# The last expert's rows added by TensorE, and the pair rows loaded behind the weights, at the end of two mixture-of-experts stages

## The reference, cut to what matters

```python
x = x + mixer(rmsnorm(x))
h = rmsnorm(x)
# g: the token's best group of 4; top-2 of the 8 experts in it; weights from both softmaxes
combine[t, expert] = weight
for e in range(32):
    hid = silu(h @ w_gate[e]) * (h @ w_up[e])            # (544, 1024) @ (1024, 256)
    out = out + combine[:, e:e+1] * (hid @ w_down[e])    # (544, 256) @ (256, 1024)
x = x + out                                              # after layer 1: rmsnorm(x) is the output
```

## Time and profile before

| | us |
|---|---|
| median of three runs (1033.27 to 1037.01) | 1036.26 |
| the profiled execution's own time | 1037.41 |
| its span in the trace | 1035.6 |
| layer 0: first gate and up of its expert stage / last copy to `rows_out` / last add to `x_T` ends | 250.49 / 485.07 / 507.81 |
| layer 1: last copy to `rows_out` / last product with the gain ends | 1002.26 / 1032.51 |

### The profile page before, as it was taken

How to read it: one execution, slowest core, us unless ns; L and a number is a source line. 1 busy time by engine, 2 the same in 40 slices (tenths; PEclk the granted TensorE clock), 3 DMA queues, 4 the chain that set the end, 5 groups by cost and what they waited for, 6 DMA issues and landing times. The chain is left out here.

```text
span 1035.6 us, 18796 instructions
## 1 busy us (share of the span) xinstructions
PE 922.1 (89%) x7270; PEld 663.2 (64%) x7270; DVE 413.8 (40%) x955; ACT 287.5 (28%) x595; POOL 293.1 (28%) x438
## 2 busy tenths in 40 slices
PE   7999999977999889876689999989979998898885
PEld 6988888864555555553587878569755555555553
DVE  5266784255111111111768878772561111111115
ACT  6356673241112111110532112362312111111103
POOL 1810000013333343311053527720123343342110
PEclk9999999997999989997699999999979999998997
DMA  8512111778999999995924636315879999999966
GB/s 234 188 37 54 49 42 53 274 293 319 379 416 416 416 414 415 418 418 199 291 67 129 159 85 155 93 43 216 358 278 390 414 417 416 416 416 418 420 270 239
DMA packets 112277, 277.71 MB, mean 268 GB/s; under 512 B 34952, under 2 KB 73176, under 8 KB 88074
## 3 DMA queue, kind: packets, MB, share of 16 engines
q1 hardware_dynamic: 96630, 253.74, 64.4%
q0 software_dynamic: 11424, 17.87, 4.7%
q10 hardware_dynamic: 4132, 4.86, 1.9%
HBM read 266.25 MB, written 27.45 MB: 284 GB/s over the span
## 5 line engine op out<-in xcount | busy, mean ns | idle before, releaser
L2106 DVE COPY areaB<-ps 128x512 f32<-128x512 f32 x66 | 45.6, 691 | 345.9 <-PE ps L2089 345.9
L2072 PE MATMUL ps<-ring,areaB 128*64 128x256 f32 x576 | 143.2, 405 | 20.7 <-issue 16.6
L2073 PE MATMUL ps<-ring,areaB 128*64 128x256 f32 x576 | 143.6, 406 | 0.0
L2118 POOL DMA_INDIRECT pair_rows<-areaB,idx x66 | 67.7, 1025 | 247.7 <-DVE areaB L2106 236.9
L2072 PEld LDWEIGHTS ps<-ring,areaB 128*64 128x64 f32 x576 | 80.9, 146 | 62.5 <-issue 23.1
L2097 ACT ACTIVATE v_rows<-ps 128x256 f32<-128x256 f32 x66 | 25.3, 384 | 257.8 <-PE ps L2073 257.8
L1058 PE MATMUL ps<-conv_x_high,pw_halves 128*128 128x272 f32 x512 | 89.4, 295 | 2.9 <-DVE areaS L1293 2.9
L2113 POOL DMA_INDIRECT areaC<-h_rows,idx x66 | 68.7, 1041 | 60.0 <-issue 45.8
L2094 ACT ACTIVATE areaB<-ps 128x512 f32<-128x512 f32 x66 | 39.3, 597 | 153.5 <-PE ps L2062 153.5
L2073 PEld LDWEIGHTS ps<-ring,areaB 128*64 128x64 f32 x576 | 80.8, 146 | 0.0
L2089 PE MATMUL ps<-ring,areaB 128*64 128x512 f32 x320 | 76.0, 593 | 2.2 <-DVE areaB L2103 1.6
(11 more groups left out here) (381 smaller groups left out, 1930.5 us busy)
## 6 DMA issues: line engine op xcount, KB each, us to landing
ring<-in_w_down SPq DMA_DIRECT2D x40, 1024.0 KB, 23.9
ring<-in_w_gate SPq DMA_DIRECT2D x32, 1024.0 KB, 23.1
ring<-in_w_up SPq DMA_DIRECT2D x32, 1024.0 KB, 26.0
wring<-in_w_down SPq DMA_DIRECT2D x12, 1024.0 KB, 25.0
areaS<-in_w_down SPq DMA_DIRECT2D x12, 1024.0 KB, 27.1
wring<-in_w_pw SPq DMA_DIRECT2D x24, 512.0 KB, 4.5
areaA<-in_w_gate SPq DMA_DIRECT2D x10, 1024.0 KB, 27.1
areaA<-in_w_up SPq DMA_DIRECT2D x10, 1024.0 KB, 29.5
```

Of the source, the lines that this page charges most:

```text
L2072: pe.matmul(ps[0:CAP, 2 + odd, 0:F], rows, ring_gate(ws)[:, k, :], start=(k == 0), stop=(k == KT - 1))
L2073: mm = pe.matmul(ps[CAP:P, 2 + odd, 0:F], rows, ring_up(ws)[:, k, :], start=(k == 0), stop=(k == KT - 1))
L2106: return v.tensor_copy(rows_out[:, s, :], ps[:, 5 + odd, :])
L2118: return gp.indirect_dma_start(pair_half_rows, bass.IndirectOffsetOnAxis(idx[:, RING + s:RING + 1 + s], 0), rows_out[:, s, :], None, bound ...
```

## The change

1. **Tile 32 isn't scattered.** Its 64 rows stay in SBUF (`late_rows`), and TensorE adds them in the combining. For this VectorE, once per layer at tile 10 (`weigh_late`, 20 instructions), takes the pairs of the last expert out of `weight` and builds a matrix from slot to token that holds their weights; TensorE turns it in tiles 12 and 14 (`turn_late`), and ScalarE keeps it in `late_T` (64 slots, twice, by 544 tokens).
2. **Order of the weights.** Down of position 30 is issued ahead of gate and up of position 31, and TensorE does down of tile 31 ahead of gate and up of tile 32 (in layer 1 also `turn_x` of two token tiles).
3. **Pairs behind the weights.** `pair(t)` now lies in weight buffers 0 and 2 alone. SP issues the loads as soon as down of tile 31 is done and the scatters of tiles 0 to 31 have landed (`early_rows_stored`), ahead of the branch for overfull experts.
4. **The combining.** Layer 0: per token tile 8 matmuls add the last expert's rows in PSUM, then 8 matmuls with the identity, in place of 8 transposes, add the mixed row. Layer 1: ScalarE and VectorE mix the two choices of the first four tiles into one row in SBUF (`mix`), TensorE adds stream and last expert in PSUM, VectorE adds both (`add_up`); only the last token tile keeps the product with the diagonal.
5. Since rows of `pair_rows` now stay unwritten, the attention stage fills it once with `x` (six transfers from DRAM to DRAM, 4.25 MB).

```diff
                     for i in range(6, NW):
                         sp.wait_ge(w_ready[i % 2], i // 2)
                         load_weights(sp, i)
+                        if i < 10:
+                            c, a = (i - 6) // 2, (i - 6) % 2
+                            sp.dma_start(pair_rows[c * T + a * NP // 2:c * T + (a + 1) * NP // 2, :],
+                                         x_prompt2[a * NP // 2:(a + 1) * NP // 2, :]).then_inc(pairs_filled, 16)
...
-        pairs = flat[:, 0:NT * 2 * D].rearrange("p (t c n) -> p t c n", t=NT, c=2)
+        pair = lambda t: ring[:, 0 if t < 3 else 2, (t % 3) * 2 * D:(t % 3 + 1) * 2 * D].rearrange("p (c n) -> p c n", c=2)
...
                 def tensor(self, pe):
-                    pe.wait_ge(out_kept, NCH)
-                    for i, t in enumerate(ORDER):
-                        r = rows_of(t)
-                        pe.wait_ge(mixed, i + 1)
+                    def late(i):
...
                         for k in range(KT):
-                            mm = pe.transpose(banks(i)[:, k // 4, (k % 4) * P:(k % 4) * P + r],
-                                              x_rows[0:r, t, k * P:(k + 1) * P], ident[0:r, 0:r])
+                            at = slice(k // 4 * CAP, (k // 4 + 1) * CAP)
+                            pe.matmul(banks(i)[:, k // 4, (k % 4) * P:(k % 4) * P + r], late_rows[at, (k % 4) * P:(k % 4 + 1) * P],
+                                      late_T[at, t * P:t * P + r], start=(k % 4 == 0), stop=False)
+
+                    def turn(i):
+                        t = ORDER[i]
+                        r = rows_of(t)
+                        pe.wait_ge(mixed, i + 1)
+                        for k in range(KT):
+                            mm = pe.matmul(banks(i)[:, k // 4, (k % 4) * P:(k % 4) * P + r],
+                                           pair(t)[0:r, 0, k * P:(k + 1) * P], ident[0:r, 0:r], start=False, stop=(k % 4 == 3))
                         mm.then_inc(turned, 1)
+
+                    pe.wait_ge(late_kept, 2)
+                    pe.wait_ge(out_kept, NCH)
+                    for i in range(4):
+                        late(i)
+                    turn(0)
+                    turn(1)
+                    late(4)
+                    for i in range(2, NT):
+                        turn(i)
...
+                def before_last(self, pe):
+                    self.turn_x(pe, 1)
+                    pe.wait_ge(out_kept, NCH - 1)
+                    self.turn_x(pe, 0)
...
+                        for c in range(2):
+                            at = slice(c * CAP, (c + 1) * CAP)
+                            mm = pe.matmul(banks(i)[0:r, c, :], late_T[at, t * P:t * P + r], late_rows[at, :], start=False, stop=i < NT - 1)
...
                         this = expert
+                        if e + 2 == NE:
+                            next_down(e, this)
                         if e + 1 < NE:
...
-                        next_down(e, this)
+                        if e + 2 != NE:
+                            next_down(e, this)
...
+                    sp.wait_ge(down_done, last)
+                    sp.wait_ge(early_rows_stored, 1)
+                    load_pairs(sp, l)
                     more.sync(sp, spill_of(sp))
-                    sp.wait_ge(rows_complete, 1)
-                    load_pairs(sp, l)
...
-                        store(Tile(e))
-                    spilled = spill_of(gp)
+                        if e < last:
+                            store(Tile(e))
                     for s in range(RROW):
-                        gp.wait_ge(scattered[s], 16 * len(range(s, NCH, RROW)))
-                    more.gpsimd(gp, spilled)
-                    gp.sem_inc(rows_complete, 1)
+                        gp.wait_ge(scattered[s], 16 * len(range(s, last, RROW)))
+                    gp.sem_inc(early_rows_stored, 1)
...
+                        if final:
+                            out(x.shift(-1))
+                            combine.before_last(pe)
...
+                        n.link(v.tensor_tensor(late_weight, late_weight, weight, ALU.mult))
+                        n.done(v.tensor_tensor(weight, weight, late_weight, ALU.subtract))
+                        for c in range(2 * NT):
+                            n.done(v.tensor_scalar(twice[:, c % NT, c // NT, :], slot_no[:, :], rank[:, c:c + 1], late_weight[:, c:c + 1],
+                                                   ALU.is_equal, ALU.mult))
```

More of the change, by code:

```diff
@@ L1972, in turn_x, with scalar, scale_first @@
+                def scalar(self, act):
+                    def scale_first(i):
                         t = ORDER[i]
                         r = rows_of(t)
[L1974 to L1980 removed]
+                        act.wait_ge(landed[t], 16)
+                        nc.scalar.activation(pair(t)[0:r, 0, :], pair(t)[0:r, 0, :], ACT.Copy,
+                                             scale=weight[0:r, t:t + 1]).then_inc(first_scaled, 1)
+                    for i in range(3):
+                        scale_first(i)
@@ L2106, in keep_out, with turn_late @@
                 return v.tensor_copy(rows_out[:, s, :], ps[:, 5 + odd, :])
+            def turn_late(pe, ts):
+                pe.wait_ge(late_step, LATE_STEPS)
+                after(pe, late_kept, ts[0] // 4)
+                for t in ts:
+                    twice = match[0:rows_of(t), 2 * t:2 * t + 2, :].rearrange("p a s -> p (a s)")
+                    mm = pe.transpose(ps[:, 7, (t % 4) * P:(t % 4) * P + rows_of(t)], twice, ident[0:rows_of(t), 0:rows_of(t)])
+                return mm
             def fill_idx(gp, s, e, sem_, of, at):
@@ L2370, in over, with before, behind @@
                                 body(e, NE * j + e, j)
-                def sync(self, sp, spilled):
+                        if behind:
+                            behind()
+                        else:
+                            for t in ORDER:
+                                eng.wait_ge(pairs_landed[l][t], 32)
+                def sync(self, sp, spilled):
+                    def before():
+                        for t in ORDER:
+                            sp.wait_ge(pairs_landed[l][t], 16)
+                    def behind():
+                        sp.wait_ge(o["complete"], 1)
+                        load_pairs(sp, l)
                     def body(e, n, j):
@@ L2376, in body @@
                             sp.dma_start(dst, rows_by_partition(src, l, e)).then_inc(o["landed"], 16)
-                    self.over(sp, spilled, body)
+                    self.over(sp, spilled, body, before=before, behind=behind)
                 def gpsimd(self, gp, spilled):
```

184 lines of the change are left out of this document (123 added, 61 removed).

## The result

| | before | changed |
|---|---|---|
| median of six runs each | 1036.63 us | 1028.89 us |
| ratio, 95% interval | | 0.9926 [0.9905, 0.9947] |
| the same again, with its own runs of before beside it (f2 below) | 1036.22 us | 1030.47 us, 0.995 [0.9929, 0.9971] |
| span of the profiled execution | 1035.6 us | 1025.5 us |

The first measurement gives 7.7 us, the second 5.8; their intervals overlap from 0.9929 to 0.9947. The two profiles lie 10.1 apart, so they are a slow and a fast example of their kinds, and no part of their difference may be read off as the gain of that part without the other runs beside it.

A forecast was written before the change was run, and what follows sets the result against it. Weights set the expert stages' pace; the serial waits behind the last weights set the end. Layer 1's -5.9 and layer 0's -2.0 sum to -7.9: 1037.41 becomes 1029.5, and the median, 1.15 lower, 1028.4 us; range 1024.5 to 1035.

The forecast's parts named there:

- the scatter's 5 us: Layer 1: tile 31's scatter takes 5 us from start to pairs issued, at 1002.2 (bounds 999.7 and 1005.9).
- -5.9: Layer 1's end: early pairs start VectorE's chain sooner, so the span ends at 1029.7 instead of 1035.6.
- The last scatter's place: End of layer 1: TensorE's new order makes the last copy end 3.8 us later, at 1006.8.
- -2.0: Layer 0's end: last add at 505.8 instead of 507.81, with TensorE late rather than the pairs.
- Granted clock 1.00 from 487 to 504: Layer 0's tail: a sign of being right, TensorE at full clock throughout its last products.
- The last one is usable at 496.9: Layer 0: pairs issued at 483.3, 6.0 us earlier, so the last pair can be used at 496.9.
- the fifth mix is done at 502.7: Layer 0's tail: the fifth mix ends at 502.7, then turn 4 at 504.5 and the add at 505.8.
- Edits costed at nothing: Both layers: added wait for reordered weights, about 5 us of weighing, and the 4.25 MB fill, all taken as hidden.
- Late scatter: Rival, layer 1: tile 31's scatter queues behind the weights, pairs at 1005.9, total -4.6, 1031.7 us; chance 0.16.
- Switches of tiling: Rival, TensorE: some 12 switches to and from 64-row products cost 0.18 each, 2.2 us, total 1030.6; chance 0.08.
- It doesn't do what it says: Rival: early pairs find another wait (ring buffers, the branch), only a small remainder stays, 1034 us; chance 0.08.
- Slower, layer 0 at half clock: Rival, layer 0's tail: new products run at 1.2 GHz, layer 0 ends 14.9 later, total +9, 1045.3 us; chance 0.08.

The follow-up runs named there:

- f2: The changed kernel again, unaltered, measured with its own runs of the kernel before: 1030.47 us, 0.995.
- e5: The kernel before with only the six fills of `pair_rows` added: 1036.75 us, 1.0008.
- e3: The changed kernel with the weighing of the last expert's slots at tile 22 instead of tile 10: 1030.81 us, 0.9939.
- e4: The changed kernel with all tiles of `turn_x` behind the last down, none ahead of the last gate and up: 1031.17 us, 0.9941.
- g1: The kernel before with only the new order of the weights: 1040.04 us, 1.0042.
- e8: The changed kernel with diagonal products for the last two token tiles of layer 1 instead of one: 1029.22 us, 0.9928.
- e1: The changed kernel, but the pairs are issued only when the last expert's copy is done as well: 1038.27 us, 1.0022.
- e2: The changed kernel with the weights' transfers in the old order, TensorE's order kept new: 1037.92 us, 1.0024.
- e7: The changed kernel with layer 0's last-expert 64-row halves in turn and the convolution's first transfers held until the fifth pair landed: 1030.39 us, 0.9949.
- f1: The changed kernel with the edits of e7 and e8 together: 1028.63 us, 0.992.

## Why the prediction was right, and where it was not

1028.4 was forecast, 1028.89 measured, and 1030.47 in the second measurement. Step by step:

- **Layer 1: the mechanism and nearly all its times held.** The old profile's copy 30 came 4.87 us later, so the forecast times less 4.87 are to be compared. Down of tile 31: 988.4 forecast, 988.46 measured. End of `turn_x`: 994.1, and 990.33 + 3.92 = 994.25. Last copy: 1001.9, and 1002.20. Scatter of tile 31: 992.0, and 991.98. Pairs: 997.3, and 997.08; the scatter's 5 us, taken between the ends 2.7 and 6.7, was 5.1 (996.85 + 5 is 1001.85, not the 1002.2 of the forecast; nothing hangs on it). Second pair scaled: 1004.2, and 1003.19 + 1.15 = 1004.34. End of the last finish: 1021.7, and 1022.40. The 0.7 is the third pair, used 3.47 us behind the second (2.6 was taken from layer 0), for which VectorE idled 1.06. So -5.9 became -5.2 between the two profiles. Against e5 it is -4.0, since the old order's own end varies; against the mean of these two, 39.63, the four profiles with an unchanged layer 1 end (changed, f2, e3, e4: mean 35.08) give -4.6.
- **What layer 1's gain is made of.** From the pairs' issue to the last finish the three old profiles take 25.85, 24.50 and 22.93 us (before, e5, g1). They differ in a half-clock spell of TensorE, for which VectorE waits: 6.8 us in the kernel before, 3.4 in e5, none in g1. In the changed kernel the clock is 1.00 until TensorE is done. Without a spell the old end would stand at about 14.4 + 22.9 = 37.3 behind copy 30 (an estimate, with g1's stretch), 2.3 more than the new one. By this estimate the change is worth 2.3 us against an old order at full clock, and the other half of the 4.6 are spells that the new order didn't have. The forecast took the one old profile, with the longest spell, as given. The same 16 records behind the same pause, in the kernel before and in g1 (TensorE):

```profile
1013.76 3.78 PE L1975 MATMUL ps<-ident,x_T 128*128 128x128 f32 x16 [1.44 <-DVE ring L2008]
```

```profile
1018.19 2.05 PE L1975 MATMUL ps<-ident,x_T 128*128 128x128 f32 x16 [1.44 <-DVE ring L2008]
```

- **The last scatter's place is bought, not free, as forecast:** the last copy comes 4.1 us later against copy 30 (14.83 for 10.71; 3.8 was forecast), and nobody waits for it, as e4 shows.
- **Layer 0: the gain came from another place.** -2.0 was forecast for the stretch behind copy 30. There the five profiles with the new layer 0 (changed, f2, e3, e4, e8) have 31.07 to 33.96, mean 32.2, against 31.82 and 33.21 of the old: nothing that can be told. The pairs did go out early (8.1 behind copy 30 for 13.3), 5.2 us and not 6.0: weights were still landing, and from the scatter of tile 31 to the pairs it took 3.5, not 2.71 (4.3 in e4, 4.8 in f2). Two steps failed behind that.
  - "Granted clock 1.00 from 487 to 504": in the changed kernel, e3 and e4 it fell to 0.50 in turn 1 (at 490.2 in the changed kernel), and turns 0 and 1 took 4.84 us, not 2.9. Half of that is a wrong cost: at full clock, in f2, the two took 3.95, as turn 0, of 32 tokens, needs 1.9 like the others and not 1.0. Together they took back what `late` saved, which was cheaper than costed (4.84 for four tiles, not 6.6, the halves overlapping in part).
  - "The last one is usable at 496.9": this took the pairs' spacing of 2.6 from the kernel before; now the fifth comes 5.0 behind the fourth and is in use 25.3 behind copy 30, not 20.9. In the forecast it would have waited 3.4 us for VectorE, whose add behind turn 2 sets "the fifth mix is done at 502.7". In the changed kernel, e3 and e4 pair and VectorE are ready within 0.1 us of each other; in f2 and e8, where the clock held in turns 0 and 1, VectorE idles 1.7 us for the pair, TensorE 2.5, and the last turn is at half clock. So it was one or the other that ate the gain. The next stage's weights stand behind the pairs in both kernels, and in the three old profiles the fifth comes 2.9 to 3.1 behind the fourth; why they hold it up more now stays open. The time of issue isn't the reason: e1 and e2, whose pairs go out 11.1 and 12.5 behind copy 30, have 5.0 and 4.9 too.
- **What was not forecast at all:** 2.1 to 4.5 us *ahead* of copy 30 in layer 0. All three profiles of the old kind have a longer wait for gate and up of tile 31 and half clock behind it, the ten of the new kind have not. I had taken the old profile's stretch as given on both sides. Counted from the layer's first copy the difference is smaller: copy 30 starts 211.7 to 214.5 us later in the three old profiles and 209.9 to 211.6 in the ten new ones, 2.0 less on the mean, since copy 29 itself comes later in some of the new ones. TensorE begins gate and up of tile 31 at 204.5 to 206.1 in both, so the weights are no later in the old order; what costs is the half clock, 7.1 to 8.4 us from there to copy 30 instead of 5.4. What removes it stays open. It isn't the order of the weights alone (g1), nor the fill (e5), nor the tile at which the weighing stands (e3, which still has 7.85). That leaves the weighing as such, the different use of banks, or what the chip's transfers do; none of these was tried.
- **Edits costed at nothing** cost nothing: the fill (e5), the weighing (moving it changes nothing, e3; 5.5 us on VectorE for the 5 that were estimated), the later halves of the last gate and up (TensorE goes from `turn_x` to them without a wait).
- **The rivals.** *Late scatter:* no; 5.1 us, not 8.5. *Switches of tiling:* in layer 1 a tile of `turn_x` and the last expert's product takes 1007.43 - 1004.39 = 3.04 us with two switches, for 1.87 + 0.95 = 2.82 without (0.95 is the estimate from down's records), so about 0.11 a switch, on an engine that isn't the bound. The 0.18 of the forecast was a wrong reading: 0.40 is the length of a record and 0.22 the distance of two starts; records that follow no switch have 0.38. The Trainium skill, "TensorEngine Tiling (Array Packing)", Key Properties, has a drain at such a switch; these rows agree with a small one. *It doesn't do what it says:* no; in layer 1 the early pairs find no other wait. *Slower, layer 0 at half clock:* the mechanism is real, in small: 3.4 us of half clock in most profiles (490 to 494 in the changed kernel, 502 to 506 in f2), 1.5 us on the last turn where it falls there, but not the 7.9 us of work that would have turned the sign.
- **Sums of the forecast that don't come out.** With the fifth pair at 496.9 and scaling, mix, turn and add behind it (1.15 + 1.27 + 1.87 + 1.25) layer 0's best case is 502.4, -5.4 and not -2.8, and both layers at their best give 1024.1. With 1.86 for each product of the last expert TensorE's side of layer 1 ends at 1023.6, not 1020.4; measured was 1.06 from one start to the next.

So the forecast total was met with one term short by a quarter (layer 1, 4.4 to 4.6 for 5.9), one that wasn't there (layer 0's end, -2.0), and one of like size that nobody had counted (layer 0 ahead of copy 30). That the sum fits is in part luck, and the second measurement, 5.8, shows how much of it may be.

## What to carry to other kernels

At the end of a stage that waits for memory, look for the one item that everything queues behind: if the last of 33 pieces can take another road (here 64 rows through TensorE), the other 32 can be collected while it is still being made, and that, not the saved transfer, is what e1 shows to pay. Such a change is a set: the transfers' order, the engine's order and the collecting only pay together; the transfers' order alone was a loss (g1, 1.0042), and without it, or without the early collecting, nothing was left (e2 1.0024, e1 1.0022). When a term rests on a spacing of transfers, don't carry it over unasked: here the same transfers stood behind the pairs, and the last one still came 5.0 us behind instead of 2.9. Before you take an old profile's end as given, read the clock in it, and take a second profile. And of an engine that now reaches a wait earlier, ask what its clock does in it.

## What was unexpected on the chip

- TensorE's clock fell in or just behind single pauses of the tail: after idling 2.47 us (f2) the next 16 records took 3.56 us, after 0.90 us (changed) 2.05 us; after a stall of 4.45 us (e2) eight records took 3.50 us, not 1.94. A pause can thus cost more than its length. The pause alone doesn't say: behind 1.44 us the clock fell in the kernel before and held in g1, and in the changed kernel it fell at 490.2 with TensorE at work without a pause since 482.59, mostly on products of 64 and of 32 rows. Why it fell there stays open.
- A pair of 1 MB that shares the queue with the next stage's weights came 5.0 us behind the one before it in the changed kernel and 2.9 to 3.1 in the old ones, without them 2.5 (e7: 498.44 - 495.94; f1 the same).
- Last scatter to pairs issued: 5.1 us with the last weights on the way (layer 1; 3.5 to 4.8 in layer 0), 2.5 to 2.9 with an idle queue (before, e2, e5, g1); the medians of all scatters, with weights flowing, are 6.7 and 6.8.
- The old order's own end of layer 1 varied by 1.3 us between two executions, with the length of TensorE's half-clock spell in it (6.8 and 3.4 us).
